# Stick-breaking scores on both halves of the array rows, from copies of keys and queries on the other 64 partitions

## The reference

```
z = einsum(q, k) * 64 ** -0.5                  # scores, [query, key]
allowed = (key < query) & valid
log_1mb = where(allowed, log_sigmoid(-z), 0)
after   = reverse cumulative sum of log_1mb over keys, without the own one
a       = where(allowed, exp(log_sigmoid(z) + after), 0)
out     = a @ v
```

## Time and profile before

| | us |
|---|---|
| median of 3 runs | 1258.5 |
| lowest and highest run | 1258.48, 1260.6 |
| the profiled execution | 1258.14 |
| its span | 1256.3 |
| TensorE matmuls busy | 1197.4 (95%) |
| ACT, VectorE, GpSimd busy | 509.7, 481.0, 465.4 |

### The profile page before, as it was taken

How to read it: one execution, slowest core, us unless ns; L and a number is a source line. 1 busy time by engine, 2 the same in 40 slices (tenths; PEclk the granted TensorE clock), 3 DMA queues, 4 the chain that set the end, 5 groups by cost and what they waited for, 6 DMA issues and landing times.

```text
span 1256.3 us, 21307 instructions
## 1 busy us (share of the span) xinstructions
PE 1197.4 (95%) x9094; PEld 990.6 (79%) x9094; DVE 481.0 (38%) x933; ACT 509.7 (41%) x883; POOL 465.4 (37%) x288
## 2 busy tenths in 40 slices
PE   8999999898989899999999999889999999999998
PEld 7998878786879578767677777669978888888886
DVE  4799233434343552533352565361432100222000
ACT  6456224242423344677435535341543322244210
POOL 3352535143514124333232522233154544344541
PEclk9999989999999999999999999999999999999999
DMA  6222323031312132111521221142132333223330
GB/s 239 85 88 75 126 69 117 27 115 61 111 36 68 36 117 70 34 34 44 212 85 60 71 83 51 53 165 85 35 107 94 118 101 101 69 99 101 117 117 34
DMA packets 33343, 110.18 MB, mean 88 GB/s; under 512 B 4049, under 2 KB 6065, under 8 KB 32610
## 3 DMA queue, kind: packets, MB, share of 16 engines
q1 hardware_dynamic: 25952, 92.44, 22.4%
q10 hardware_dynamic: 6786, 16.26, 3.5%
q0 software_dynamic: 512, 0.13, 0.1%
HBM read 99.43 MB, written 9.04 MB: 86 GB/s over the span
## 4 chain that ended last, share of the span: by engine, by line
PE 76%; DVE 12%; ACT 6%; issue 3%; POOL 2%; DMA 1%; ACTq 0%; DVEq 0%
PE pst L1715 17%; PE pst L1716 15%; PE pst L1717 15%; PE pst L1892 5%; PE pst L1894 5%; PE pst L1893 5%; ACT w_hi L843 1%; PE pst L2202 1%; PE pst L2194 1%; PE pst L1931 1%; PE pst L1918 1%; PE pst L2179 1%; POOL rw_m L802 1%; PE pst L2165 1%; PE pst L1984 1%
## 5 line engine op out<-in xcount | busy, mean ns | idle before, releaser
L725 POOL TENSOR_TENSOR w_lo<-raw,w_hi 128x1024 fp32r<-128x1024 f32 x164 | 399.5, 2441 | 646.2 <-ACT w_hi L843 634.5
L1715 PE MATMUL pst<-h_hi,w_hi 128*128 128x512 f32 (+1 forms) x704 | 255.9, 364 | 1.4 <-DVE h_lo L1288 0.7
L1717 PE MATMUL pst<-h_hi,w_lo 128*128 128x512 f32 (+1 forms) x704 | 244.1, 347 | 0.0
L1716 PE MATMUL pst<-h_lo,w_hi 128*128 128x512 f32 (+1 forms) x704 | 243.8, 346 | 0.0
L843 ACT ACTIVATE w_hi<-raw 128x1024 fp32r<-128x1024 f32 x164 | 171.3, 1051 | 149.0 <-PE pst L1894 114.2
L1715 PEld LDWEIGHTS pst<-h_hi,w_hi 128*128 128x128 f32 x704 | 133.9, 190 | 25.4 <-issue 4.3
L1716 PEld LDWEIGHTS pst<-h_lo,w_hi 128*128 128x128 f32 x704 | 134.2, 191 | 15.8 <-issue 2.2
L1717 PEld LDWEIGHTS pst<-h_hi,w_lo 128*128 128x128 f32 x704 | 133.8, 190 | 16.3
L1715 PE MATMUL pst<-x_hi,w_hi 128*128 128x512 f32 (+1 forms) x272 | 103.1, 379 | 3.8 <-POOL w_lo L725 2.0
L1717 PE MATMUL pst<-x_hi,w_lo 128*128 128x512 f32 (+1 forms) x272 | 103.0, 379 | 0.0
L1716 PE MATMUL pst<-x_lo,w_hi 128*128 128x512 f32 (+1 forms) x272 | 103.0, 378 | 0.0
(11 more groups left out here) (335 smaller groups left out, 2166.6 us busy)
## 6 DMA issues: line engine op xcount, KB each, us to landing
raw<-in_weights SPq DMA_DIRECT2D x164, 512.0 KB, 3.4
xt<-in_x SPq DMA_DIRECT2D x4, 512.0 KB, 5.3
wait_gate<-stage ACTq DMA_DIRECT2D x8, 256.0 KB, 2.1
gate_t<-wait_gate ACTq DMA_DIRECT2D x1, 2048.0 KB, 8.3
x<-in_x ACTq DMA_DIRECT2D x1, 2048.0 KB, 8.4
out<-x SPq DMA_DIRECT2D x8, 256.0 KB, 3.4
cst<-in_consts SPq DMA_DIRECT2D x1, 1524.0 KB, 11.0
wait_ret_v<-stage ACTq DMA_DIRECT2D x8, 128.0 KB, 2.0
```

The costliest lines, as they stand in the source:

```text
L725: nc.gpsimd.tensor_tensor(w_lo[:, u % W_SLOTS, :], raw[:, u % RAW_SLOTS, :], w_hi[:, u % W_SLOTS, :].bitcast(F32), ALU.subtract).then_inc( ...
L1715: M(out, lh, rh, start=(first and i == 0), stop=False)
L1716: M(out, lh, rl, start=False, stop=False)
L1717: last = M(out, ll, rh, start=False, stop=(final and i == len(terms) - 1))
```

## The change

From head 1 on, blocks 1 and 3 are computed on the other half of the array's rows. For that the head's keys of these two blocks, and its queries from the second block on, are copied to the other 64 partitions: `swap_halves(t)` does it for the two heads of tile t, with four DMAs from ACT's queue (for each direction one for the keys, in two stretches of 128, and one for 384 columns of queries). Tiles 0 and 1 are copied in `reload_early`, tiles 2 and 3 at the end of ACT's `sb_z` of heads 1 and 3, into the same two buffers (`sb_kx`, `sb_qx`). The buffers lie where constants of the RWKV stage were, and behind `sb_s_hi1`. TensorE waits for the copies by `swap_in` ahead of the scores. Block 3 moves from bank 6 to bank 5, behind block 1, and the columns of the softplus tiles are ordered to match (`SB_COL`); what read the two banks as 2 x 384 columns now reads 768 in a row. Several semaphores are merged: `mix_tanh` and `rg_tanh` into `tanh_done`, `sg_ready` into `par_ready`, `sb_kmd_ready` and `dk2_own` into `keys_copied`, with the counts raised to match.

```diff
@@ -308,7 +308,7 @@
-        SB_COL = [0, T, 2 * T - P, 3 * T - 3 * P]
+        SB_COL = [0, T, 2 * T, 2 * T - P]
...
@@ -324,6 +324,10 @@
+        at = [SBUF_BASE + 4 * CONST_AT["rw_mask"][0]]
+        sb_qx = place("sb_qx", [P, 2, T - P], at=at)
+        sb_kx = [place("sb_kx0", [P, 2 * P], at=at), place("sb_kx1", [P, 2 * P], at=[top + 4 * (SB_N - T)])]
+        assert at[0] <= SBUF_BASE + 4 * CONST_AT["suffix"][0] and SB_N - T + 2 * P <= 2 * T
...
@@ -412,7 +417,7 @@
-        mix_tanh, sg_ready = sem("mix_tanh"), sem("sg_ready")
+        tanh_done = sem("tanh_done")
...
@@ -444,7 +449,7 @@
-        sb_kmd_ready, sb_vmd_ready = sem("sb_kmd_ready"), sem("sb_vmd_ready")
+        keys_copied, sb_vmd_ready = sem("keys_copied"), sem("sb_vmd_ready")
...
@@ -529,7 +534,9 @@
-            return tile[:, SB_COL[2] - P:SB_N].rearrange("p (a b) -> p a b", a=2)[:, :, P:2 * P]
+            return tile[:, SB_COL[3]:SB_COL[3] + 2 * P].rearrange("p (a b) -> p a b", a=2)
+
+        sb_rest = pst[:, 5:7, :].rearrange("p a b -> p (a b)")[:, 0:SB_N - T]
...
@@ -968,6 +975,9 @@
                 act.dma_start(gate_t[:], spill["rgate"]).then_inc(gates_in, 16)
+                act.wait_ge(*all_out("aq", ("aq", 3, 0)))
+                swap_halves(0)
+                swap_halves(1)
...
@@ -1024,7 +1034,7 @@
-                return tile[:, 0:T], tile[:, T:SB_N].rearrange("p (a b) -> p a b", a=2)
+                return tile[:, 0:T], tile[:, T:SB_N]
...
@@ -1032,6 +1042,13 @@
                 A(sb_mask_r[:, 2 * P:], C("carry_meta"), ACT.Copy).then_inc(s_hi, 1)
+
+            def swap_halves(t):
+
+                for to, at_ in ((slice(0, HD), slice(HD, P)), (slice(HD, P), slice(0, HD))):
+                    act.dma_start(sb_kx[t % 2][to, :].rearrange("p (a b) -> p a b", a=2),
+                                  sb_k[at_, t, MB:].rearrange("p (a b) -> p a b", a=2)[:, :, P:2 * P]).then_inc(swap_in[t % 2], 16)
+                    act.dma_start(sb_qx[to, t % 2, :], sb_q[at_, t, P:T]).then_inc(swap_in[t % 2], 16)
 
...
@@ -1041,10 +1058,12 @@
                 act.wait_ge(z_done, 2 * h + 2)
-                link(A(e1, pst[:, 5:7, 0:3 * P], ACT.Abs))
+                link(A(e1, sb_rest, ACT.Abs))
                 A(e0, e0, ACT.Ln, bias=1.0).then_inc(z_ln, 1)
                 link(A(e1, e1, ACT.Exp, scale=-1.0))
                 A(e1, e1, ACT.Ln, bias=1.0).then_inc(z_ln, 1)
+                if h in (1, 3):
+                    swap_halves((h + 3) // 2)
 
...
@@ -1059,7 +1078,7 @@
-                A(e1, pst[:, 5:7, 0:3 * P], ACT.Exp).then_inc(z_a, 1)
+                A(e1, sb_rest, ACT.Exp).then_inc(z_a, 1)
...
@@ -1319,8 +1338,8 @@
-            dve.wait_ge(mix_tanh, 2)
-            V.tensor_scalar(SG[:], SG[:], 1.0, 0.5, ALU.add, ALU.mult).then_inc(sg_ready, 1)
+            dve.wait_ge(tanh_done, 2)
+            V.tensor_scalar(SG[:], SG[:], 1.0, 0.5, ALU.add, ALU.mult).then_inc(par_ready, 1)
...
@@ -1433,15 +1452,15 @@
-                V.scalar_tensor_tensor(out=halves(sb_s[:, T:SB_N]), in0=pst[:, 5:7, 0:3 * P], scalar=0.0,
-                                       in1=halves(e[:, T:SB_N]), op0=ALU.max, op1=ALU.add).then_inc(z_sp, 1)
+                V.scalar_tensor_tensor(out=sb_s[:, T:SB_N], in0=sb_rest, scalar=0.0, in1=e[:, T:SB_N],
+                                       op0=ALU.max, op1=ALU.add).then_inc(z_sp, 1)
 
             def sb_sums(h):
 
                 dve.wait_ge(s_hi, 2 * h + 2)
                 V.tensor_tensor(sb_s_lo[:, 0:T], sb_s[:, 0:T], sb_s_hi[0][:].bitcast(F32), ALU.subtract).then_inc(s_lo, 1)
                 dve.wait_ge(z_spm, 2 * h + 2)
-                s1, s2, s3 = sb_s[:, SB_COL[1]:SB_COL[2]], sb_s[:, SB_COL[2]:SB_COL[3]], sb_s[:, SB_COL[3]:SB_N]
+                s1, s2, s3 = (sb_s[:, SB_COL[kb]:SB_COL[kb] + SBW[kb]] for kb in (1, 2, 3))
...
@@ -1900,23 +1919,31 @@
                 if grp == 0:
-                    pe.wait_ge(sb_kmd_ready, SBH)
+                    pe.wait_ge(keys_copied, SBH)
                 else:
                     pe.wait_ge(zm_a, grp)
                 for t in (2 * grp, 2 * grp + 1):
                     last = M(pst[:, 7, :], sb_kmd[:, t, :], sb_q[:, t, :], start=(t == 2 * grp), stop=(t == 2 * grp + 1))
                 last.then_inc(zm_done, 1)
 
-            SB_AT = [(4, 0), (5, 0), (6, 0), (6, 2 * P)]
+            SB_AT = [(4, 0), (5, 0), (6, 0), (5, 3 * P)]
 
             def sb_z(h):
                 r = sb_rows(h)
+                t, other = h // 2, sb_rows(h + 1)
+                if h:
+                    pe.wait_ge(swap_in[t % 2], 16 * 4 * (t // 2 + 1))
                 for kb in range(NB):
                     if h and kb < 2:
                         pe.wait_ge(z_a, 2 * h - 1 + kb)
                     bank, c = SB_AT[kb]
-                    last = M(pst[:, bank, c:c + T - P * kb], sb_k[r, h // 2, MB + P * kb:MB + P * kb + P],
-                             sb_q[r, h // 2, P * kb:T], start=(kb < 3), stop=True, skip_group_check=(kb == 3))
+                    if h and kb in (1, 3):
+                        keys = sb_kx[t % 2][other, P * (kb // 2):P * (kb // 2) + P]
+                        queries = sb_qx[other, t % 2, P * (kb - 1):T - P]
+                    else:
+                        keys, queries = sb_k[r, t, MB + P * kb:MB + P * kb + P], sb_q[r, t, P * kb:T]
+                    last = M(pst[:, bank, c:c + T - P * kb], keys, queries,
+                             start=(kb < 3), stop=True, skip_group_check=(kb == 3))
                     if kb in (0, NB - 1):
...
```

More of the change, by code:

```diff
@@ L398, in build @@
         const_in, table_in = sem("const_in"), sem("table_in")
+        swap_in = [sem(f"swap_in{i}") for i in range(2)]
         xb_in = [sem(f"xb_in{b}") for b in range(NB)]
@@ L454, in build @@
         s_hi, s_lo, cs_ready, cs_split = sem("s_hi"), sem("s_lo"), sem("cs_ready"), sem("cs_split")
-        rg_tanh, rqd_ready = sem("rg_tanh"), sem("rqd_ready")
+        rqd_ready = sem("rqd_ready")
         rkt_done, rkd_ready, rs_done, rsc_ready, rkv_done, rstate, ro_done, ro_ready = (
@@ L460, in build @@
         rsq_ready, rss_done, rrs_ready, ry_ready = sem("rsq_ready"), sem("rss_done"), sem("rrs_ready"), sem("ry_ready")
-        dsq_ready, dss_done, drs_ready, dn_ready, dk2_own, dk2_in = (
-            sem("dsq_ready"), sem("dss_done"), sem("drs_ready"), sem("dn_ready"), sem("dk2_own"), sem("dk2_in"))
+        dsq_ready, dss_done, drs_ready, dn_ready, dk2_in = (
+            sem("dsq_ready"), sem("dss_done"), sem("drs_ready"), sem("dn_ready"), sem("dk2_in"))
         ds_done, ds_read, dmx_ready, dexp_ready, dp_ready, dpt_done, dpt_act, dpt_dve, do_done = (
@@ L1077, in ret_gate @@
                 act.wait_ge(ret_g_in, 16)
-                A(rth[:], rg[:], ACT.Tanh, scale=0.5).then_inc(rg_tanh, 1)
+                A(rth[:], rg[:], ACT.Tanh, scale=0.5).then_inc(tanh_done, 1)
                 use_tables("natural_log_exp_and_others")
@@ L1196, in _ @@
             act.wait_ge(c_mixed, 1)
-            A(WA[0:HD, :], WA[0:HD, :], ACT.Tanh).then_inc(mix_tanh, 1)
+            A(WA[0:HD, :], WA[0:HD, :], ACT.Tanh).then_inc(tanh_done, 1)
             act.wait_ge(c_mixed, 2)
-            A(SG[:], SG[:], ACT.Tanh, scale=0.5).then_inc(mix_tanh, 1)
+            A(SG[:], SG[:], ACT.Tanh, scale=0.5).then_inc(tanh_done, 1)
             act.wait_ge(par_ready, 3)
@@ L1422, in sb_keys @@
                     V.tensor_copy(sb_kmd[r, h // 2, MB * (h % 4):MB * (h % 4) + MB], sb_k[r, h // 2, 0:MB])\
-                        .then_inc(sb_kmd_ready, 1)
+                        .then_inc(keys_copied, 1)
             def sb_meta(grp):
@@ L1469, in ret_gate @@
                                     ALU.mult).then_inc(rqd_ready, 1)
-                dve.wait_ge(rg_tanh, 1)
+                dve.wait_ge(tanh_done, 3)
                 V.scalar_tensor_tensor(out=rg[:], in0=rth[:], scalar=1.0, in1=rg[:], op0=ALU.add, op1=ALU.mult)
@@ L1521, in sw_keys @@
                     own = slice(HD * kv, HD * kv + HD)
-                    V.tensor_copy(dk2[own, kv, :], dk[own, :]).then_inc(dk2_own, 1)
+                    V.tensor_copy(dk2[own, kv, :], dk[own, :]).then_inc(keys_copied, 1)
             def sw_scores(i):
@@ L1782, in lora @@
                 if t == 0:
-                    pe.wait_ge(mix_tanh, 1)
+                    pe.wait_ge(tanh_done, 1)
                     pe.wait_ge(table_in, 32)
@@ L2063, in sw_scores @@
                     pe.wait_ge(dn_ready, 5)
-                    pe.wait_ge(dk2_own, 2)
+                    pe.wait_ge(keys_copied, SBH + 2)
                     pe.wait_ge(dk2_in, 32)
@@ L2285, in _ @@
             pe.wait_ge(yy_copied, 2 * NB)
-            pe.wait_ge(sg_ready, 1)
+            pe.wait_ge(par_ready, 5)
             def post_sum(t):
```

## The result

| | before | after |
|---|---|---|
| median of 17 runs, us | 1258.48 (1256.01 to 1261.60) | 1261.59 (1257.81 to 1264.81) |
| profiled execution: time / span, us | 1258.14 / 1256.3 | 1261.59 / 1259.6 |
| stick-breaking stage, us | 142.71 | 144.55 |

The ratio is 1.0023, 95% interval 1.0013 to 1.0034: slower by about 2.9 us (1.6 to 4.3). The forecast was 1260.0 with a range of 1257 to 1262.6.

What follows compares the result with a forecast made beforehand. Each head was taken as bound by two routes of nearly one length, TensorE's work and the softplus chain. Terms -0.64 + 1.70 + 0.41 gave +1.5 us, hence 1259.6, or 1260.0 as median; range 1257 to 1262.6.

Steps and rivals of the forecast that it cites:

- mark of 2.5 us: Whole kernel: a difference under 0.2%, 2.5 us, can't be told from no change; faster 0.10, same 0.65, slower 0.25.
- Scores 2.42 to 1.8 us: Score matmuls of heads 1 to 7: two row halves at once save some 0.6 us each, limited by block 1's bank.
- Odd heads gain 0: Heads 1, 3, 5, 7: the softplus chain on ACT caps them, so shorter scores bring 0.
- Even heads -0.33, -0.31, 0: Heads 2, 4, 6: value products wait for GpSimd's mask, capping the gains at 0.33, 0.31 and 0 us.
- Heads 1 and 3, 4x - 1.63 each: Four copy issues between L1047 and L1051 on ACT delay the score arguments by 0.85 us in each head, +1.70 together.
- x: Mean time one copy issue holds ACT's queue, taken as 0.62 us, with 0.07 added for the key copies' third dimension.
- Heads 5 and 7, wait 0.2 to 0.7: Sign in the profile after: TensorE's wait for L1055 grows from 0.2 to some 0.7 us in these heads.
- Start of the stage +0.41: Eight issues on ACT move head 0's work by 4.96 us, of which 0.41 us reaches TensorE through VectorE's late eviction.
- The merged semaphores and the waits, 0: Merged semaphores add no instruction, and waits for the copies stand ahead of one where TensorE idles anyway: 0.
- Rival A: TensorE's time counts and copies hide: 0.6 us from each of seven heads, -4.2, time 1254.3; chance 0.08.
- Rival B: Issues on ACT are dearer, x from 0.68 to 0.88, at the top +5.6 us, 1264.1; chance 0.23.
- Rival C: Row halves don't run at once or copies cost nothing: -0.6 to +2.1 us; counted within the forecast's 0.69.

Runs made afterwards that it cites:

- the array alone: Changed kernel without any copies or waits for them; blocks 1 and 3 use the wrong head's data on the other row half: 1257.89 us, ratio 0.9995 to before.
- the copies alone: Changed kernel with all sixteen copies and TensorE's waits, but every score block on its original row half: 1262.28 us, ratio 1.0028 to the kernel before.
- SP's issues: Changed kernel with the same sixteen copies issued from SyncE's queue instead of ACT's: 1257.91 us, ratio 1.0000 to the kernel before.
- SP's issues and one fill moved: Changed kernel with copies issued from SyncE's queue and one fill piece moved ahead of the value products between heads 5 and 6: 1257.95 us, ratio 0.9992 to before.

## Why the prediction was right

The mechanism held: ACT's queue, held by the issues at two places, costs more than two capped gains bring. The stage came out at +1.84 for +1.47. The median, 1261.59, is 1.6 above the forecast's 1260.0, and only 0.4 of that is the stage; that it fell into the range owes to the range's width, 5.6 us. Against the prediction's own mark of 2.5 us the measured 2.9 is on the slow side, to which it had given 0.25 and not 0.65, though the interval, 1.6 to 4.3, reaches below the mark. By term:

- *Scores 2.42 to 1.8 us:* 1.74 in head 1. The bound by block 1's bank holds: its weight load waited 0.34 for L1081 and started 0.61 behind the first matmul (0.70 before). In the array alone it started 0.70 behind, and the scores took 1.83; in both they end 1.13 us after that weight load.
- *Odd heads gain 0:* nearly. L1061 starts 1.17 after L1058, not 1.30: the scores' end had held it by that little. So 0.1 to 0.14 a head (the array alone). That ACT's chain keeps most of the rest was tested by cutting it.
- *Even heads -0.33, -0.31, 0:* measured -0.27, -0.31, 0 in after, -0.30, -0.33, 0 without the copies. Shown by the waits for GpSimd's mask, and for head 6 by taking the split away ahead of it.
- *Heads 1 and 3, 4x - 1.63 each:* the formula gives 0.99 at 0.655 us an issue; measured 0.98 and 0.99 with the copies alone, and 0.84 and 0.90 in the changed kernel, after the gain of 0.1 that I had left out. L1070 starts 2.65 after L1064; the prediction's list of signs has 3.1 there, but its own terms make 0.06 + 4x + 0.04 = 2.58. TensorE's wait did not stand at L1074 alone: 0.40 at L1070, 0.36 in the first arguments, where a weight load waited 0.43 for L1461, and 0.65 at L1074 (0.2 before): 1.4 together, where 1.5 was forecast for L1074.
- *Heads 5 and 7, wait 0.2 to 0.7:* 0.48 for L1072 and 0.36 for L1074, so 0.8, and at another place in part. Waits view, TensorE, 455 to 625 us, of after (us in total, times, longest):

```profile
PE pst L1734 <- DVE sb_v L1402: 2.4, 1, 2.4
PE pst L1945 <- ACT sb_e L1079: 2.2, 7, 0.3
PE pst L1958 <- ACT sb_cs_hi L1074: 1.4, 4, 0.5
PE pst L1958 <- ACT sb_s_hi L1070: 0.9, 2, 0.5
```

- *The term that was mis-sized is x,* the cost of one issue, 0.62. The group of issues (ns: lowest, median, longest) and the step of 0.655 in head 1 say why:

```profile
L1049 ACTq DMA_DIRECT2D sb_kx<-sb_k x8: 623/626/705, 460.3 to 531.6; - x8
L1051 ACTq DMA_DIRECT2D sb_qx<-sb_q x8: 622/627/825, 461.1 to 532.3; - x8
```

  The instruction itself takes what I gave it; the gap of 0.03 to the next I had left out. The third dimension, for which I had added 0.07 to the key copies, costs nothing: keys and queries are equal. With 0.655 the formula gives 16 x 0.655 - 8.45 = +2.0 in place of +1.5, measured +1.84.
- *Start of the stage +0.41:* +0.83, +0.89 and +0.68 in the three profiles of the changed kernel. Eight issues took ACT from 460.3 to 465.90 (the last one, L1051, began at 465.08 and took 0.82), 0.70 each: some 0.6 later than with 0.62, of which 0.42 reached TensorE. That this interval follows the issues one for one is shown with the copies alone, where they took 5.94. VectorE's L1455 (in after the counterpart of L1436) came at 471.88, the eviction behind it at 472.76, and TensorE waited 2.37 us for it. Timeline of after:

```profile
460.55 1.92 DVE L1441 COPY sb_kmd<-sb_k 64x32 f32<-64x32 f32 x8 [0.63 <-POOL sb_kmd L739]
...
466.00 1.06 ACT L850 ACTIVATE w_hi<-raw 128x1024 fp32r<-128x1024 f32 x1 [8.56 <-issue]
467.14 2.39 POOL L732 TENSOR_TENSOR w_lo<-raw,w_hi 128x1024 fp32r<-128x1024 f32 x1 [6.16 <-ACT w_hi L850]
...
471.88 0.96 DVE L1455 SCALAR_TENSOR_TENSOR sb_s<-pst,sb_e 128x768 f32<-128x768 f32 x1 [0.92 <-ACT sb_e L1064]
472.76 0.75 DVE L1402 COPY sb_v<-pst 128x256 f32<-128x256 f32 x2
473.23 0.39 PE L1734 MATMUL pst<-w_hi,h_hi 128*128 128x256 f32 x1 [2.37 <-DVE sb_v L1402]
```

  Part of that wait is not new: before, TensorE waited 1.61 us at another place of this interval, for an eviction behind VectorE's key copies. That wait is gone: GpSimd's split now comes after those copies, and none of them stands for it (last section). So the net is 0.83 and not 2.4. Two timeline rows of before:

```profile
457.96 4.02 DVE L1422 COPY sb_kmd<-sb_k 64x32 f32<-64x32 f32 x8 [0.62 <-POOL sb_kmd L732]
...
462.49 0.39 PE L1715 MATMUL pst<-w_hi,h_hi 128*128 128x256 f32 x1 [1.61 <-DVE sb_vm L1381]
```

- *The merged semaphores and the waits, 0:* not quite. TensorE starts the scores 0.31 after L1079's release instead of 0.22, and 0.22 again in the array alone, which has no such wait. That is 0.09 a head, but block 1's bank sets the end of the scores either way (0.31 + 1.74 = 0.22 + 1.83), so little of it arrives: with SP's issues and this wait the stage is 0.27 longer than in the array alone, the traffic of the copies included. It was left out of the sum, as was the gain of 0.1 in the odd heads, and by luck the two nearly cancel.

Rival A, that TensorE's time counts, falls: scores 4.1 us shorter brought 1.05. Rival B has the forecast's mechanism; its price, 0.68 to 0.88 an issue, came only at the start (0.70), not in heads 1 and 3 (0.655). Rival C falls in both halves: the scores did get shorter (2.42 to 1.74), and the copies cost 2.65 us of stage where they stand. By the Trainium skill's TensorEngine Tiling (Array Packing), Overview, a contraction of 64 gives up to twice the speed. Here it was 2.42 / 1.74 = 1.4 times, of which the late bank explains a part: without it the longer half alone would take 1.45 by the prediction's estimate.

**What stays open.** The stage explains 1.84, 1.87 and 1.66 us in the three profiles. The times say more: over 39 runs of the changed kernel and 112 of the one before the means differ by 2.9, give or take 0.7. Part of that goes with TensorE's granted clock, which is known for all 39 and for 95 of the 112. At a mean of 0.994, 7 runs of the changed kernel took 1258.89 in the mean and 23 of the other 1257.16, 1.7 less; at 0.991 they differ by 2.3 (10 and 22 runs), at 0.990 by 2.8 (8 and 18). A straight line through all of them, with one slope for both kernels, puts the changed kernel 2.3 us over the other at equal clock, give or take 0.3. So some 0.5 us is left outside the stage, and 0.6 goes with the lower mean clock of its runs (0.9910 against 0.9918, a difference only just clear of noise). Why it is lower stays open. What such a run contains can be seen in the windows view at other places (us; busy and count of PE, PEld, DVE, ACT, POOL; granted clock; DMA share; GB/s), first after, then before:

```profile
795.00:805.00 10.00, 7.40 (x31) 6.04 (x31) 6.07 (x16) 1.47 (x5) 0.86 (x1) 0.83 0.17 54
830.00:840.00 10.00, 7.87 (x28) 5.95 (x27) 7.71 (x10) 2.89 (x5) 3.66 (x2) 0.83 0.52 177
```

```profile
705.00:715.00 10.00, 8.72 (x54) 7.15 (x51) 7.88 (x25) 4.64 (x13) 6.75 (x10) 0.83 0.27 93
895.00:905.00 10.00, 8.20 (x57) 7.99 (x56) 6.37 (x24) 5.93 (x21) 0.00 (x0) 0.83 0.01 2
```

In each TensorE was idle for 1.3 to 2.6 us, and part of the window was granted 1.2 instead of 2.4 GHz, 0.17 x 10 = 1.7 us of clock lost. By the line above, whose slope is 0.63 us of time for each us of clock lost, such a place costs about 1.1 us (an estimate). Three of the places, at 795, 830 and 410, are in the profile of after and not in that of before, but also in those of kernels that were no slower (the 795 and 830 ones in the last with SP's issues and one fill moved). Whether the changed kernel meets them more often can't be said from three profiles of it and one of the other.

## What to carry to other kernels

Before making a busy engine faster, read in each repetition of the loop which wait ends last: at 95% busy, score matmuls 4.1 us shorter were worth 1.05. Count a DMA issue as an instruction of the queue that issues it, with its gap to the next, and put it where that engine waits anyway; four issues in an odd head cost 0.9 to 1.0 us, the same four in an even head or on SP none. Compare times at equal granted clock where runs differ in it: it took the give or take of this comparison from 0.7 to 0.3 us. When one cover goes, name the next engine in line (here GpSimd's split ahead of a mask) before moving more work under it.

## What the runs showed of the hardware

- An issue of a copy between partition halves held the queue for 0.62 us on ACT and 0.60 to 0.62 on SP, single ones up to 0.97 (the copies alone), where one plain load took 0.33. It overlapped the running ACTIVATE, but not the next.
- VectorE's eight small copies took 4.02 us beside GpSimd's 128x1024 subtraction and 1.92 in after, where that came later. All of the difference is one copy. It began 0.15 us after GpSimd's instruction (458.94, 2.39 us), took 2.27 us and ended 0.03 after it; the seven others took what they take in after, and GpSimd's instruction took 2.39 in both. So VectorE did not slow down there: one instruction stood until GpSimd's had ended. Timeline of before, the copy and GpSimd's instruction:

```profile
458.94 2.39 POOL L725 TENSOR_TENSOR w_lo<-raw,w_hi 128x1024 fp32r<-128x1024 f32 x1 [0.54 <-ACT w_hi L843]
459.09 2.27 DVE L1422 COPY sb_kmd<-sb_k 64x32 f32<-64x32 f32 x1
```

  The group of copies (ns: lowest, median, longest), before and after:

```profile
L1422 DVE COPY sb_kmd<-sb_k x8: 173/179/2275, 458.0 to 461.8; 64x32 f32<-64x32 f32 x8
L1441 DVE COPY sb_kmd<-sb_k x8: 174/178/465, 460.5 to 462.3; 64x32 f32<-64x32 f32 x8
```

- With a second wait ahead of it the first matmul started 0.31 us after the release instead of 0.22, though what the second waited for had long landed.
- A stretch at the lower granted clock lost 1.7 us of clock, at places that changed from execution to execution. Runs of one kernel spread over 5 to 8 us, and the granted clock goes with it: 0.63 us of time for each us of clock lost, over 134 runs.
